# Two 128x256 matmuls in place of each 128x512 matmul of the three MLPs

## The chip, the cores and the metric

The kernel runs on one core of a Trainium2 chip (eight cores, one used). The metric is the device time of one execution in microseconds (us), taken as the median of several runs. A program is slower or faster here only if its time moves by more than about 0.2%, which is 4.6 us.

## What is computed

The reference is two small transformer blocks, one after the other, in float32, on 512 tokens of width 1024. The first block has an RWKV-7 recurrence beside differential attention, then a cross attention to 256 memory tokens, then an MLP. The second has two layers: a gated linear attention with an MLP, and a sliding-window attention with an MLP. The change touches only the three MLPs, which all have this form:

```python
D_FF = 4 * D_MODEL            # 4096
hn = rms_norm(h, norm_mlp_w[l])
h = h + jnp.square(jax.nn.relu(hn @ w_up[l])) @ w_down[l]
```

So each MLP is a product [512 x 1024] x [1024 x 4096], a squared ReLU, and a product [512 x 4096] x [4096 x 1024].

## The kernel before

**Layout.** Activations lie transposed: 128 features on the partitions, 512 tokens (`T`) along the row, with `KT` = 8 such tiles for a width of 1024. A matmul takes a 128x128 tile of the weights as its stationary operand and 128x512 of the activations as its moving operand, and adds 128 output features for all 512 tokens into one PSUM bank (128x512 float32, a whole bank). There are four banks `M[0..3]` for such products.

**Precision.** Each float32 operand is split in two parts, `_hi` and `_lo`, of the type fp32r. `exact3` (L1079 to L1082) makes one product from three matmuls: w_hi x x_hi, w_lo x x_hi, w_hi x x_lo. So a *triple* of matmuls stands for one 128x128 tile of weights.

**Weights.** SyncE loads the weights in blocks of 256 columns for eight k-tiles (1 MB) into a ring of four `raw` buffers (L964). ScalarE makes `w_hi` of a block (L1390), VectorE makes `w_lo` (L1606), each in a ring of two.

**The MLP on TensorE** (`mlp`, from L1128). It goes over the hidden width in two halves (loop `half`). In each half, first the up stage: a hardware loop `j` of two turns, four blocks of weights in each, two chunks `c` of 128 columns in each block. A chunk is eight k-tiles of three matmuls, that is 24 matmuls into one bank, from `f_hi` and `f_lo`, and its last matmul increments `acc_done`. VectorE then takes the ReLU out of the bank (L1677), ScalarE squares it (L1433) and makes `u_hi` (L1435), VectorE makes `u_lo` (L1680). Then the down stage: a hardware loop `q` of two turns with four blocks each; a bank takes 24 matmuls in a block for k-group 0, and 24 more in a later block for k-group 1, before VectorE adds it to `h` (L1692, L1701). On each engine the code's order is the order of work; TensorE waits for semaphores at the start of a block (`block_ready`, weights split) and of a chunk (`bank_free`, bank emptied).

All in all an MLP has 2 halves x (2 turns x 4 blocks x 2 chunks + 2 turns x 4 blocks x 2 chunks) x 24 = 1536 matmuls, and the three have 4608.

**Other matmuls that the prediction speaks of.** `chunk` is the same scheme outside the MLPs; for the memory tokens it runs with 256 tokens, `blocks(N_MK, 4, m_hi, m_lo, ..., tok=MEM)`. `block_tm` (matmuls L1113 to L1115) turns the roles round: 128 tokens of the activations are stationary and 256 columns of the weights move. `mem_scores` calls `exact3` with the queries `mq` stationary and 256 memory tokens `mk` moving, into one half of a bank and then the other. `norm_stat` (L1122) sums squares with a 128x512 matmul before each MLP.

Of the kernel before, what the change touches and what calls it, by code (L numbers as in the profile page):

```python
# [19 lines left out]
P = 128  # L20
T = 512
D = 1024
KT = D // P
# [88 lines left out]
def acc_before(n):  # L112

    return 2 * n - 16 * sum(n >= m + 32 for m in (N_MLP1, N_MLP2, N_MLP3))
# [20 lines left out]
def program(nc, A, out):  # L135
# [4 lines left out]
    with ctx:  # L140
# [17 lines left out]
        def at(off, name, shape, dt=f32):  # L158
            nbytes = 4 * int(np.prod(shape[1:]))
            t = nc.alloc_sbuf_tensor_at(name, shape, dt, offset=off[0])  # L160
            off[0] += (nbytes + 31) // 32 * 32
            return t
# [4 lines left out]
        w_hi = at(o, "w_hi", [P, 2, KT, BW], f32r)  # L167
        w_lo = at(o, "w_lo", [P, 2, KT, BW], f32r)
# [136 lines left out]
        def C(name, rows=slice(0, P)):  # L305
            a, n = CONST[name]
            return cst[rows, a:a + n]
# [756 lines left out]
        def _(pe):  # L1064
            mm = nc.tensor.matmul

            def wait(name, v):
                pe.wait_ge(S[name], v)

            def bank_free(k, r=None):  # L1070

                if k >= 4:
                    pe.wait_ge(S["acc_evac"], k - 3 if r is None else k - 3 + r)
                return M[k % 4]

            def block_ready(n, r=None):
                pe.wait_ge(S["w_lo_ready"], n + 1 if r is None else n + 1 + r)

            def exact3(dst, wh, wl, xh, xl, start, stop):  # L1079
                mm(dst, wh, xh, start=start, stop=False)  # L1080
                mm(dst, wl, xh, start=False, stop=False)  # L1081
                return mm(dst, wh, xl, start=False, stop=stop)  # L1082

            def chunk(n, c, hi, lo, first=None, cols=P, tok=T, inc=1, lo_sem="x_lo", order=range(KT)):

                if c == 0:
                    block_ready(n)
                k = acc_before(n) + c
                dst = bank_free(k)
                for i, kt in enumerate(order):  # L1090
                    if first is not None:
                        wait(lo_sem, first + i + 1)
                    ws = slice(c * P, c * P + cols)
                    last = exact3(dst[0:cols, 0:tok], w_hi[:, n % 2, kt, ws], w_lo[:, n % 2, kt, ws],
                                  hi[:, kt, 0:tok], lo[:, kt, 0:tok], i == 0, i == KT - 1)
                last.then_inc(S["acc_done"], inc)
# [31 lines left out]
            def mlp(n, first, nth):  # L1128
                f_hi, f_lo, u_hi, u_lo = mem_of[nth]
                k = acc_before(n)  # L1130
                with pe.Fori(0, 2) as half:
                    with pe.Fori(0, 2) as j:
                        for b in range(4):
                            block_ready(n + b, half * 16 + j * 4)
                            for c in range(2):
                                dst = bank_free(k + 2 * b + c, half * 24 + j * 8)
                                for kt in range(KT):
                                    if b == 0 and c == 0:
                                        wait("x_lo", first + kt + 1)
                                    ws = slice(c * P, c * P + P)  # L1140
                                    last = exact3(dst[:], w_hi[:, (n + b) % 2, kt, ws], w_lo[:, (n + b) % 2, kt, ws],
                                                  f_hi[:, kt, :], f_lo[:, kt, :], kt == 0, kt == KT - 1)
                                last.then_inc(S["acc_done"], 1)
                    with pe.Fori(0, 2) as q:
                        for b in range(4):
                            kg = b // 2
                            m = n + 8 + b
                            block_ready(m, half * 16 + q * 4)

                            pe.wait_ge(S["up_lo"], 32 * nth + 8 * kg + 8 + half * 16)  # L1150
                            for c in range(2):
                                kk = k + 16 + 2 * (b % 2) + c
                                dst = M[kk % 4] if kg else bank_free(kk, half * 24 + q * 4)
                                for kt in range(KT):
                                    ws = slice(c * P, c * P + P)
                                    last = exact3(dst[:], w_hi[:, m % 2, kt, ws], w_lo[:, m % 2, kt, ws],
                                                  u_hi[:, kg * 8 + kt, :], u_lo[:, kg * 8 + kt, :],
                                                  kg == 0 and kt == 0, kg == 1 and kt == KT - 1)
                                last.then_inc(S["acc_done"], 1)


# [1 line left out]
            for g in range(4):  # L1163
                wait(f"ld_x{g}", 16)
                for c in (2 * g, 2 * g + 1):
                    if c >= 4:
                        wait("xt_ev", c - 3)
                    for t in range(TT):
                        last = nc.tensor.transpose(X[c % 4][:, t * P:t * P + P], xt[:, t, c * P:c * P + P], C("ident"))
# [25 lines left out]
            for u in range(16):  # L1195
# [4 lines left out]
                for m in range(2):  # L1200
                    r = slice(64 * m, 64 * m + 64)
                    last = mm(X[m][:, 0:nk], dq[r, hd, qb * P:qb * P + P], dk[r, hd, 0:nk], start=True, stop=True)
# [11 lines left out]
                for kb in range(qb + 1):  # L1214
                    last = nc.tensor.transpose(X[2][:, kb * P:kb * P + P], de[1][:, kb * P:kb * P + P], C("ident"))
# [4 lines left out]
                for kb in range(qb + 1):  # L1220
                    last = mm(X[3][:, qb * P:qb * P + P], dv[:, kb, hd * P:hd * P + P], da_t[:, kb, :],  # L1221
                              start=kb == 0, stop=kb == qb)
# [13 lines left out]
            for g in range(4):  # L1236
                for i in range(2):
                    for t in range(2):
                        c = 2 * g + i
                        last = nc.tensor.transpose(X[g][:, i * MEM + t * P:i * MEM + t * P + P],  # L1240
                                                   mrow[:, t, c * P:c * P + P], C("ident"))
# [29 lines left out]
            for hd in range(4):  # L1271
# [5 lines left out]
                for t in range(2):  # L1277
                    for qb in range(4):
                        last = nc.tensor.transpose(X[2 + t][:, qb * P:qb * P + P], me[hd % 2][:, qb, t * P:t * P + P],
                                                   C("ident"))  # L1280
# [5 lines left out]
                for i in range(2):  # L1286
                    for t in range(2):
                        wait("ma_pt_lo", 2 * hd + t + 1)
                        f = slice((2 * hd + i) * P, (2 * hd + i) * P + P)
                        last = exact3(M[i], mv_hi[:, t, f], mv_lo[:, t, f], pt_hi[:, t, :], pt_lo[:, t, :],  # L1290
                                      t == 0, t == 1)
# [3 lines left out]

            norm_stat(2)
            mlp(N_MLP1, 16, 0)
            norm_stat(3)

            gla_pe(pe, mm, wait, chunk, blocks, block_tm, norm_stat)  # L1300
            norm_stat(5)
            mlp(N_MLP2, 32, 1)


# [37 lines left out]
            for c in range(KT):  # L1342
# [5 lines left out]
                for qb in range(4):  # L1348
# [7 lines left out]
                    for i in range(2):  # L1356
                        for kb in kbs:
                            last = mm(M[c % 2][64 * i:64 * i + 64, qb * P:qb * P + P],  # L1358
                                      sv[:, qb - 1 + kb, (c // 4) * 64:(c // 4) * 64 + 64],
                                      spt[u % 2][:, 2 * i + kb, :], start=kb == kbs[0], stop=kb == 1)  # L1360
                    last.then_inc(S["sw_pv"], 1)
            wait("sw_lo", KT)
            blocks(N_SOUT, 4, s_hi, s_lo)
            norm_stat(7)
            mlp(N_MLP3, 56, 2)
            norm_stat(8)

# [3 lines left out]
            for t in range(TT):  # L1371
                for half in range(2):
# [3 lines left out]
                    for c in range(4):  # L1376
                        last = nc.tensor.transpose(X[2 + i % 2][:, c * P:c * P + P], h[:, 4 * half + c, t * P:t * P + P],
                                                   C("ident"))
# [585 lines left out]
```

## Time and profile before

| | |
|---|---|
| median of 3 runs | 2297.1 us (2295.41 to 2300.19) |
| span of the profiled execution, first to last instruction | 2294.3 us |
| TensorE busy with matmuls / with weight loads | 2113.8 us (92%) / 1704.6 us (74%) |
| VectorE, ScalarE, GpSimd busy | 1006.4 us (44%), 744.2 us (32%), 114.5 us (5%) |
| mean granted TensorE clock | 0.953 of full speed |
| matmuls recorded | 13074, of them 4608 in the MLPs |

The time of the profiled execution itself is not listed beside its span; the span is 2.8 us under the median of the runs. A matmul and the loading of its weights are one instruction in the program and two records in the trace: PE is the matmul, PEld the weight load. Records of matmuls overlap, since they are pipelined: one of 395 ns starts every 232 ns. So the pace of a stretch is read from start times, and not from durations. A few matmul records are missing from the trace, so counts are taken from the loops where they matter.

### The profile page before, as it was taken

What the parts mean: (1) busy time and instruction counts of PE and PEld (TensorE: products, weight loads), DVE (VectorE), ACT (ScalarE), POOL (GpSimd) and SP (SyncE); (2) the same over time, 40 slices, a digit from 0 to 9 for tenths busy, and PEclk for the clock granted to TensorE, in tenths of its full rate; (3) what the DMA queues carried; (4) which work ended last, traced back from release to release, by engine and by line L of the source; (5) the groups of instructions that cost most, each with busy time, mean ns of one, the idle gap of its engine ahead of it and who ended that gap; (6) DMA issues with size and microseconds to landing.
All of it is one profiled execution on the core that took longest, in us unless ns stands there. A gap on an engine that the chain in (4) does not pass through costs nothing.

```text
span 2294.3 us, 31118 instructions
## 1 busy us (share of the span) xinstructions
PE 2113.8 (92%) x13074; PEld 1704.6 (74%) x13074; DVE 1006.4 (44%) x1274; ACT 744.2 (32%) x1083; POOL 114.5 (5%) x85
## 2 busy tenths in 40 slices
PE   6998688889989999997989899999999789999997
PEld 5865477669777888884787778888888567888885
DVE  4365355356444423425443444324343644423433
ACT  3132333244233312323322333223232553312321
POOL 2044000000000000002000000000000310000000
PEclk8999599989999999997999999999999799999999
DMA  6211000025262232221221022222232012222220
GB/s 193 92 56 55 1 3 3 3 74 167 80 90 88 92 110 91 92 74 55 92 92 56 19 86 97 92 91 92 91 124 93 5 37 92 92 92 91 92 92 37
DMA packets 167206, 176.22 MB, mean 77 GB/s; under 512 B 4045, under 2 KB 164838, under 8 KB 167105
## 3 DMA queue, kind: packets, MB, share of 16 engines
q1 hardware_dynamic: 165072, 167.79, 22.6%
q0 software_dynamic: 2032, 6.98, 1.9%
q8 instruction: 76, 1.25, 0.2%
q14 instruction: 26, 0.21, 0.0%
HBM read 169.51 MB, written 5.24 MB: 76 GB/s over the span
## 4 chain that ended last, share of the span: by engine, by line
PE 87%; DVE 6%; ACT 5%; issue 1%; DMA 0%; POOL 0%; SPq 0%; DVEq 0%; ACTq 0%
PE M L1080 23%; PE M L1081 23%; PE M L1082 23%; PE M L1113 1%; PE M L1115 1%; PE M L1114 1%; PE X L452 1%; PE M L452 1%; PE M L1358 1%; ACT sc L1573 1%; ACT mt L500 1%; PE X L1335 1%; PE X L1221 1%; PE X L760 1%; DVE h L1661 1%
## 5 line engine op out<-in xcount | busy, mean ns | idle before, releaser
L1606 DVE TENSOR_TENSOR w_lo<-raw,w_hi 128x2048 fp32r<-128x2048 f32 x155 | 353.2, 2278 | 364.9 <-ACT w_hi L1390 364.9
L1390 ACT ACTIVATE w_hi<-raw 128x2048 fp32r<-128x2048 f32 x155 | 293.6, 1895 | 407.9 <-PE M L1082 364.0
L1080 PE MATMUL M<-f,w_hi 128*128 128x512 f32 x768 | 304.6, 397 | 0.0
L1081 PE MATMUL M<-f,w_lo 128*128 128x512 f32 x768 | 303.4, 395 | 0.0
L1082 PE MATMUL M<-f,w_hi 128*128 128x512 f32 x768 | 303.3, 395 | 0.0
L1082 PE MATMUL M<-u,w_hi 128*128 128x512 f32 x768 | 303.1, 395 | 0.0
L1081 PE MATMUL M<-u,w_lo 128*128 128x512 f32 x768 | 303.1, 395 | 0.0
L1080 PE MATMUL M<-u,w_hi 128*128 128x512 f32 x768 | 303.1, 395 | 0.0
L1080 PEld LDWEIGHTS M<-f,w_hi 128*128 128x128 f32 x768 | 144.8, 189 | 35.4 <-issue 1.3
L1081 PEld LDWEIGHTS M<-f,w_lo 128*128 128x128 f32 x768 | 144.7, 188 | 34.8 <-issue 0.5
L1082 PEld LDWEIGHTS M<-f,w_hi 128*128 128x128 f32 x768 | 144.7, 188 | 34.2
L1081 PEld LDWEIGHTS M<-u,w_lo 128*128 128x128 f32 x768 | 144.5, 188 | 34.3
L1080 PEld LDWEIGHTS M<-u,w_hi 128*128 128x128 f32 x768 | 144.5, 188 | 34.2
L1082 PEld LDWEIGHTS M<-u,w_hi 128*128 128x128 f32 x768 | 144.5, 188 | 34.1
L1433 ACT ACTIVATE nt<-ut 128x512 f32<-128x512 f32 x96 | 60.7, 632 | 323.6 <-DVE ut L1677 323.6
L1680 DVE TENSOR_TENSOR u<-nt,u 128x512 f32 x96 | 66.5, 692 | 153.3 <-ACT u L1435 153.3
L1399 ACT ACTIVATE nt<-h 128x512 f32<-128x512 f32 x72 | 45.5, 631 | 246.2 <-DVE h L1630 112.2
L1677 DVE SCALAR_TENSOR_TENSOR ut<-M,rstd 128x512 f32<-128x512 f32 x96 | 66.1, 688 | 105.2 <-PE M L1082 105.0
L1080 PE MATMUL M<-gx_hi,w_hi 128*128 128x512 f32 (+1 forms) x200 | 82.2, 411 | 15.4 <-DVE gx_lo L1643 9.9
L1080 PE MATMUL M<-xm_hi,w_hi 128*128 128x512 f32 x176 | 72.6, 412 | 10.2 <-issue 10.2
L1082 PE MATMUL M<-gx_lo,w_hi 128*128 128x512 f32 (+1 forms) x200 | 81.8, 409 | 0.0
L1081 PE MATMUL M<-gx_hi,w_lo 128*128 128x512 f32 (+1 forms) x200 | 81.7, 409 | 0.0
(483 smaller groups left out, 3342.6 us busy)
## 6 DMA issues: line engine op xcount, KB each, us to landing
raw<-in_w_up_dram SPq DMA_DIRECT2D x48, 1024.0 KB, 5.3
raw<-in_w_down_dram SPq DMA_DIRECT2D x48, 1024.0 KB, 5.1
raw<-in_w_in_dram SPq DMA_DIRECT2D x14, 1024.0 KB, 5.4
raw<-in_a_w_in_dram SPq DMA_DIRECT2D x12, 1024.0 KB, 5.4
raw<-in_w_out_dram SPq DMA_DIRECT2D x4, 1024.0 KB, 5.0
raw<-in_w_mk_dram SPq DMA_DIRECT2D x4, 1024.0 KB, 5.0
raw<-in_w_mv_dram SPq DMA_DIRECT2D x4, 1024.0 KB, 5.2
raw<-in_w_mq_dram SPq DMA_DIRECT2D x4, 1024.0 KB, 5.1
```

The source lines that it names most:

```text
L452: last = mm(blk(bank, hh, cp, cpar), a_, b_, start=True, stop=True)
L500: nc.scalar.activation(out_, in_, func, **kw).then_inc(S["rw_act"], 1)
L760: last = mm(X[2 + hd // 2][:, (hd % 2) * 256:(hd % 2) * 256 + 256], gkt[cp % 2][r, hd, :], gv[r, cp, hd * 256:hd * 256 + 256], start=True, ...
L1080: mm(dst, wh, xh, start=start, stop=False)
L1081: mm(dst, wl, xh, start=False, stop=False)
L1082: return mm(dst, wh, xl, start=False, stop=stop)
L1390: nc.scalar.activation(w_hi[:, n % 2, :, 0:cols], raw[:, n % 4, :, 0:cols], ACT.Copy).then_inc(S["w_hi_ready"], 1)
L1399: nc.scalar.activation(b_[:, 0:tok], src, ACT.Square).then_inc(S[sem[0]], 1)
L1433: nc.scalar.activation(us[c][:], ut[c][:], ACT.Square).then_inc(S["up_sq"], 1)
L1606: TTO(w_lo[:, n % 2, :, 0:cols], raw[:, n % 4, :, 0:cols], w_hi[:, n % 2, :, 0:cols].bitcast(f32), ALU.subtract).then_inc(S["w_lo_ready"], 1)
L1677: STT(ut[c][:], M[(k + i) % 4], 0.0, rstd[:], ALU.max, ALU.mult).then_inc(S["acc_evac"], 1)
L1680: TTO(u_lo[:, u_, :], us[c][:].unsqueeze(1), u_hi[:, u_, :].bitcast(f32), ALU.subtract).then_inc(S["up_lo"], 1)
```

## The change

Each matmul of the MLPs over 512 tokens becomes two, over tokens 0 to 255 and 256 to 511. Each of the two has its own weight load. In the up stage the loop over the token halves `tk` lies outside the loop over the k-tiles: 24 matmuls into the first half of the bank and then 24 into the second. In the down stage it lies inside: three matmuls into the first half of the bank, three into the second, for each k-tile. There, only the very first matmul into a bank has `start` set. Semaphores, banks, loads and the other engines' code stay as they are.

```diff
-            def exact3(dst, wh, wl, xh, xl, start, stop):
-                mm(dst, wh, xh, start=start, stop=False)
-                mm(dst, wl, xh, start=False, stop=False)
-                return mm(dst, wh, xl, start=False, stop=stop)
+            def exact3(dst, wh, wl, xh, xl, start, stop, **kw):
+                mm(dst, wh, xh, start=start, stop=False, **kw)
+                mm(dst, wl, xh, start=False, stop=False, **kw)
+                return mm(dst, wh, xl, start=False, stop=stop, **kw)
...
-                                for kt in range(KT):
-                                    if b == 0 and c == 0:
-                                        wait("x_lo", first + kt + 1)
-                                    ws = slice(c * P, c * P + P)
-                                    last = exact3(dst[:], w_hi[:, (n + b) % 2, kt, ws], w_lo[:, (n + b) % 2, kt, ws],
-                                                  f_hi[:, kt, :], f_lo[:, kt, :], kt == 0, kt == KT - 1)
+                                for tk in (slice(0, 256), slice(256, T)):
+                                    for kt in range(KT):
+                                        if b == 0 and c == 0:
+                                            wait("x_lo", first + kt + 1)
+                                        ws = slice(c * P, c * P + P)
+                                        last = exact3(dst[:, tk], w_hi[:, (n + b) % 2, kt, ws], w_lo[:, (n + b) % 2, kt, ws],
+                                                      f_hi[:, kt, tk], f_lo[:, kt, tk], kt == 0, kt == KT - 1)
...
                                 for kt in range(KT):
-                                    ws = slice(c * P, c * P + P)
-                                    last = exact3(dst[:], w_hi[:, m % 2, kt, ws], w_lo[:, m % 2, kt, ws],
-                                                  u_hi[:, kg * 8 + kt, :], u_lo[:, kg * 8 + kt, :],
-                                                  kg == 0 and kt == 0, kg == 1 and kt == KT - 1)
+                                    for tk in (slice(0, 256), slice(256, T)):
+                                        ws = slice(c * P, c * P + P)
+                                        last = exact3(dst[:, tk], w_hi[:, m % 2, kt, ws], w_lo[:, m % 2, kt, ws],
+                                                      u_hi[:, kg * 8 + kt, tk], u_lo[:, kg * 8 + kt, tk],
+                                                      kg == 0 and kt == 0 and tk.start == 0, kg == 1 and kt == KT - 1,
+                                                      skip_group_check=True)
```

TensorE's instructions in the up stage of the first MLP, at the end of its first chunk (`f_0` is `f_hi`, `f_1` is `f_lo`; the REGISTER_ALU at L1073 works out what `bank_free` of the next chunk waits for). Before:

```order
L1080 MATMUL M<-f_0_142,w_hi 128x512
L1081 MATMUL M<-f_0_142,w_lo 128x512
L1082 MATMUL M<-f_1_143,w_hi 128x512
L1073 REGISTER_ALU
L1080 MATMUL M<-f_0_142,w_hi 128x512
```

And at the same place now:

```order
L1080 MATMUL M<-f_0_142,w_hi 128x256
L1081 MATMUL M<-f_0_142,w_lo 128x256
L1082 MATMUL M<-f_1_143,w_hi 128x256
L1080 MATMUL M<-f_0_142,w_hi 128x256
L1081 MATMUL M<-f_0_142,w_lo 128x256
```

After the 24th matmul the 25th follows, the first one over the other token half, and the next chunk comes only after the 48th. Nothing moves on the other engines, and SyncE's list is the same.

## Rows read from the trace of the kernel before

**Rows 1.** The page: TensorE's line, the chain that ended last, the MLP matmuls.
```profile
PE 2113.8 (92%) x13074; PEld 1704.6 (74%) x13074; DVE 1006.4 (44%) x1274; ACT 744.2 (32%) x1083; POOL 114.5 (5%) x85
...
PE 87%; DVE 6%; ACT 5%; issue 1%; DMA 0%; POOL 0%; SPq 0%; DVEq 0%; ACTq 0%
...
L1080 PE MATMUL M<-f,w_hi 128*128 128x512 f32 x768 | 304.6, 397 | 0.0
```

**Rows 2.** Busy time in the MLPs: engine us (instructions), granted clock, DMA share, GB/s.
```profile
705.60:1065.00 359.40, 357.30 (x1537) 289.31 (x1536) 129.64 (x119) 104.39 (x106) 0.00 (x0) 1.00 0.28 91
1353.80:1712.00 358.20, 358.20 (x1538) 290.00 (x1537) 133.48 (x122) 109.65 (x112) 0.00 (x0) 1.00 0.29 94
1915.00:2275.70 360.70, 358.55 (x1537) 288.14 (x1535) 129.41 (x118) 104.20 (x105) 0.00 (x0) 1.00 0.25 82
```

**Rows 3.** Timeline of TensorE: an early and the last matmul of each MLP.
```profile
706.03 0.39 PE L1081 MATMUL M<-f,w_lo 128*128 128x512 f32 x1
...
1062.50 0.40 PE L1082 MATMUL M<-u,w_hi 128*128 128x512 f32 x1
...
1356.18 0.39 PE L1081 MATMUL M<-f,w_lo 128*128 128x512 f32 x1
...
1711.94 0.40 PE L1082 MATMUL M<-u,w_hi 128*128 128x512 f32 x1
...
1915.22 0.39 PE L1081 MATMUL M<-f,w_lo 128*128 128x512 f32 x1
...
2273.15 0.40 PE L1082 MATMUL M<-u,w_hi 128*128 128x512 f32 x1
```

**Rows 4.** Waits in the first MLP: who waited for whom, us, times, longest.
```profile
ACT w_hi L1390 <- PE M L1082: 105.7, 12, 9.3
DVE ut L1677 <- PE M L1082: 34.4, 17, 2.6
```

**Rows 5.** Timeline: memory keys, 256 tokens moving, weights stationary (`chunk`).
```profile
531.89 0.28 PE L1080 MATMUL M<-m_hi,w_hi 128*128 128x256 f32 x1
...
544.81 0.28 PE L1080 MATMUL M<-m_hi,w_hi 128*128 128x256 f32 x1
```

**Rows 6.** Timeline: memory values (`block_tm`), around the wait at 550.7 us.
```profile
549.90 0.28 PE L1115 MATMUL M<-w_hi,m_lo 128*128 128x256 f32 x1
...
550.58 0.28 PE L1115 MATMUL M<-w_hi,m_lo 128*128 128x256 f32 x1
550.73 0.38 PE L1113 MATMUL M<-w_hi,m_hi 128*128 128x256 f32 x1
...
551.07 0.28 PE L1115 MATMUL M<-w_hi,m_lo 128*128 128x256 f32 x1
...
552.83 0.28 PE L1115 MATMUL M<-w_hi,m_lo 128*128 128x256 f32 x1
```

**Rows 7.** Tiles xm_hi and gx_hi in `block_tm`: duration ns, first and last start.
```profile
L1114 PE MATMUL M<-w_lo,xm_hi x64: 279/279/279, 76.8 to 99.1; 128*128 128x256 f32 x64
...
L1113 PE MATMUL M<-w_hi,gx_hi x80: 279/281/285, 1166.8 to 1194.9; 128*128 128x256 f32 x80
```

**Rows 8.** Timeline: `mem_scores`, one half of a bank after the other.
```profile
616.17 0.28 PE L1081 MATMUL X<-mk_hi,mq_lo 128*128 128x256 f32 x1
...
618.93 0.28 PE L1080 MATMUL M<-mk_hi,mq_hi 128*128 128x256 f32 x1
```

**Rows 9.** Timeline: 128 columns moving (`block_tm` of the shared keys and values).
```profile
1721.80 0.27 PE L1113 MATMUL M<-w_hi,kx_hi 128*128 128x128 f32 x1
...
1722.81 0.28 PE L1113 MATMUL M<-w_hi,kx_hi 128*128 128x128 f32 x1
```

**Rows 10.** Timeline: end of the first turn of loop `j`; entry to the MLP.
```profile
705.54 0.19 PEld L1080 LDWEIGHTS M<-f,w_hi 128*128 128x128 f32 x1 [0.41 <-issue]
...
750.18 0.39 PE L1082 MATMUL M<-f,w_hi 128*128 128x512 f32 x1
750.41 0.39 PE L1080 MATMUL M<-f,w_hi 128*128 128x512 f32 x1
```

## The prediction

> **What bounds the kernel now.** I read the page first. TensorE has matmuls in flight for 92% of the span, and the chain that ended last is TensorE for 87% [rows 1]. Then the busy time by stage: in the three MLPs, 1078 us of the 2294 us, matmuls are in flight 357 to 359 us out of 358 to 361, the clock is at its full level (1.00, that is 2.4 GHz), VectorE is busy 36% and ScalarE 30% [rows 2]. Nobody is ahead of TensorE there: in the waits of the first MLP ScalarE waits 105.7 us for it before it may split new weights, and VectorE waits 34.4 us for finished banks [rows 4]; no wait of TensorE stands inside an MLP. So a nanosecond more or less on each MLP matmul goes straight into the time, and all else of this change can hide. What must be known is the pace, start to start.
>
> **The pace with 512 columns.** From the second matmul of the first MLP to its 1536th are 1534 steps: (1062.50 - 706.03) / 1534 = 0.2324 us [rows 3]. In the second MLP the first row shown is the fifth matmul (a cold start lies before it): 355.76 / 1531 = 0.2324. In the third: 357.93 / 1534 = 0.2333. Over all 4608: 1536 x (0.2324 + 0.2324 + 0.2333) = 1072.3 us. These quotients hold 24 turns of the hardware loops, 192 chunks' waits and all weights, and still no step stands out: at the end of the first turn of `j` the next matmul starts 0.23 us after the last [rows 10].
>
> **What the change removes.** 4608 matmuls of 512 columns, at 1072.3 us. Nothing else: no load, no wait, no evacuation.
>
> **What it adds.** 9216 matmuls of 256 columns, with twice the weight loads. Their pace is the whole question. Break-even is 1072.3 / 9216 = 0.1164 us. The kernel already runs such matmuls, at full clock, in five places:
> - Memory keys, `chunk` with 256 tokens: 38 triples from 531.89 to 544.81, 12.92 / 114 = 0.1133 us [rows 5].
> - Memory values, `block_tm`: 6 steps in 0.68 us, 0.1133, up to the wait; 15 steps from 551.07 to 552.83, 0.1173, behind it [rows 6].
> - First projections, `block_tm`: 63 triples, 22.3 / 189 = 0.1180 [rows 7].
> - Gated attention, `block_tm`: 79 triples, 28.1 / 237 = 0.1186 [rows 7].
> - Memory scores, `exact3` into one half of a bank and then the other: 23 steps in 2.76 us, 0.1200 [rows 8].
>
> With 128 columns a step still takes 1.01 / 9 = 0.1122 us [rows 9]. There the moving operand is half as long and the step hardly shorter, so 0.112 us is what a weight load of 128 columns needs, and that is the floor below which no 256-column step can go. With 512 columns the load lies under the matmul with room to spare; with 256 the two are as long as each other, and the step is whatever their interplay makes it: from 0.1133 to 0.1200 in these rows. The break-even lies inside.
>
> Which value? Nearest by its code is the row at 0.1133: weights stationary, tokens moving, L1080 to L1082 as in the MLP. But `mem_scores` is the same function too and stands at 0.1200, and it alone writes the two halves of a bank in turn every few matmuls, as the new down stage does every three. And the memory values ran at 0.1133 and, behind one short wait, with the same code and the same tiles, at 0.1173 for good [rows 6]. So the pace seems to be something that the pipeline settles into at a start, and four of the five places settled at or above 0.117 sooner or later. I take 0.1180, the middle of these and the pace of the cleanest long stretch. Then 9216 x 0.1180 = 1087.5 us, **+15.2 us**. The ends are 9216 x 0.1133 = 1044.2 (-28.1 us) and 9216 x 0.1200 = 1105.9 (+33.6 us); they are kept for the range.
>
> Here the Trainium skill has a rule against the change. The page "TensorE: Matmul & The Clock Gate", section "Back-to-back issue gap", gives a warm step as the columns over 2.4 GHz plus about 2.5 ns. By it each added matmul costs 2.5 ns, an estimate of 11.5 us slower in all: the same sign as my sum and near its size. The trace does not bear out the rule's own figure for 512 columns, 216 ns against 0.2324 us measured.
>
> **What hides.** The other engines' work is the same in amount. A block of weights takes TensorE 48 x 0.2324 = 11.2 us now and 11.3 us then, and VectorE needs about 36% of it [rows 2]; even at 0.1133 (10.9 us) that stays far off. The banks go by the last matmul of a chunk as before, so the half that is ready earlier helps nobody. The ends of turns and the semaphore waits of a chunk cost nothing now; TensorE has half the time per instruction to cover them, and the memory keys cross four borders of chunks of 24 such matmuls at an unbroken 0.1133 us [rows 5], so I cost them at nothing. If the cover were gone, the entry to the MLP shows a price: 0.41 us of waiting for the issue [rows 10], times 24 turns, 10 us. The clock stays at its full level as matmuls stay gapless.
>
> **Sum.** Against the profiled span: 2294.3 + 15.2 = 2309.5 us. The median of the runs stands 2.8 us above that span, so the forecast is 2297.1 + 15.2 = 2312 us.
>
> **The rivals.**
> - *The quick pace holds (faster).* The MLPs settle at 0.1133 as the memory keys did, and stay there, since nothing in an MLP makes TensorE wait: 2297.1 - 28 = 2269 us. For it: same operands, same function, and a stretch of 13 us with chunk borders that never left the pace. Against it: the four other places. It decides in each MLP from the first microseconds on, wherever the step is under 0.1164. Chance 0.30.
> - *Mixed.* Some MLPs or stages (the up stage writes one half 24 times, the down stage alternates) settle at 0.1133 and others at 0.118. One MLP of three at the quick pace gives 2297.1 + (15.2 x 2 - 28.1) / 3 = 2298 us, two give 2297.1 + (15.2 - 28.1 x 2) / 3 = 2283 us. Chance 0.15.
> - *The pace of the scores everywhere.* 0.1200, for the changes of bank half: 2297.1 + 33.6 = 2331 us. Chance 0.11.
> - *The covers fall* at the turns of the loops, on top of 0.1180: 2312 + 10 = 2322 us. Against it: no mark now. Chance 0.03.
> - *Loads that no longer lie under matmuls.* Each added matmul would then cost a bare load of 0.112 us, 4608 x 0.112 = 516 us, 2813 us. The rows at 256 columns exclude it almost: a step of 0.113 to 0.120 us has no room for a load of 0.112 beside the streaming. Chance 0.01. The same page's Part 3 (row and column tiling) says that a weight load overlaps a running matmul only if its row group differs; the trace says otherwise, since all these tiles use all 128 rows and overlap.
>
> **How the numbers follow.** The forecast of 2312 us, with a pace between 0.1165 and 0.1190, has 0.40. Its own range is 2298 to 2322 us (9216 x 0.1165 and 0.1190 against 1072.3). Cases of both signs hold most of the chance, so the range must reach both ends: down to 2268 for the quick pace, up to 2334 for the pace of the scores. What lies outside (covers lost on top of 0.1200, bare loads, a pace outside the five) is under 0.1. A measurement of this kernel tells about 0.2%, 4.6 us, from no change. Faster: the quick pace 0.30 and half of the mixed case 0.08, 0.38. The same: the rest of the mixed case and the lower edge of the forecast, 0.09. Slower: 0.53.
>
> **What would show it.** In the profile after, the steps of L1080 to L1082 on `f` and `u` by their start times: 0.118 bears the forecast out, 0.1133 the first rival, 0.1200 the third. The stages must then last 9216 / 3 x the pace, 362.5 us each at 0.118. Weight loads should be in flight for all of each MLP, against 80% now (289 of 359 us). A gap at every 384th matmul would be the turns; a wait of TensorE for `w_lo` or a bank inside an MLP would prove the part on what hides wrong. A pace that changes within an MLP, or differs between up and down, would be the mixed case.

## The result, and the profile after

The changed kernel takes 2315.96 us (median of 4 runs, 2314.7 to 2324.16), the kernel before beside it 2296.26 us (4 runs, 2291.27 to 2300.19): a ratio of 1.0093, with a 95% interval of 1.0073 to 1.0114, **19.7 us slower**. The profiled execution of the changed kernel is the longest of its four, 2324.16 us, with a span of 2322.0.

The page of the changed kernel: TensorE's line, the shares of the chain, the MLP matmuls (busy us, mean ns of one, idle before them).

```profile
PE 2144.6 (92%) x17682; PEld 1941.6 (84%) x17682; DVE 1006.6 (43%) x1274; ACT 744.0 (32%) x1083; POOL 114.5 (5%) x85
...
PE 87%; DVE 6%; ACT 5%; issue 1%; DMA 0%; POOL 0%; SPq 0%; DVEq 0%; ACTq 0%
...
L1080 PE MATMUL M<-f,w_hi 128*128 128x256 f32 x1536 | 435.8, 284 | 0.0
```

These answer to [rows 1]: 4608 matmuls and weight loads more, VectorE and ScalarE unchanged, TensorE the bound as before. The busy time of each engine in the three MLPs (stretch, PE busy, PEld, DVE, ACT, POOL, granted clock, DMA share, GB/s), to be laid beside [rows 2]:

```profile
706.90:1077.00 370.10, 370.09 (x3074) 369.37 (x3072) 127.69 (x116) 103.78 (x105) 0.00 (x0) 1.00 0.28 88
1366.00:1731.00 365.00, 365.00 (x3075) 364.88 (x3074) 133.48 (x122) 109.64 (x112) 0.00 (x0) 1.00 0.29 92
1933.80:2300.10 366.30, 366.30 (x3074) 366.19 (x3072) 127.38 (x115) 103.55 (x104) 0.00 (x0) 1.00 0.25 80
```

Weight loads are in flight for the whole of each MLP (369.37 of 370.10 us, against 289 of 359), VectorE and ScalarE work as long as before, and no MLP has an idle stretch on TensorE. So nearly all of the added time is in the pace. The timeline of TensorE, an early (warm) and the last matmul of each MLP, as in [rows 3]:

```profile
709.03 0.28 PE L1081 MATMUL M<-f,w_lo 128*128 128x256 f32 x1
...
1076.71 0.28 PE L1082 MATMUL M<-u,w_hi 128*128 128x256 f32 x1
...
1366.43 0.28 PE L1081 MATMUL M<-f,w_lo 128*128 128x256 f32 x1
...
1730.74 0.28 PE L1082 MATMUL M<-u,w_hi 128*128 128x256 f32 x1
...
1937.63 0.28 PE L1082 MATMUL M<-f,w_hi 128*128 128x256 f32 x1
...
2300.02 0.28 PE L1082 MATMUL M<-u,w_hi 128*128 128x256 f32 x1
```

Of the 3072 matmuls of an MLP, the first rows shown are the 8th, the 2nd and the 18th. First MLP: (1076.71 - 709.03) / 3064 = 0.1200 us. Second: 364.31 / 3070 = 0.1187. Third: 362.39 / 3054 = 0.1187. Break-even was 0.1164. The pace is the same in the up stage, in the down stage and across the turns of the loops.

**Where the 27.7 us of span went.** At these paces the 9216 matmuls take 3072 x (0.1200 + 0.1187 + 0.1187) = 1098 us against 1072.3 before: 25.7 us. About 1.5 us more is a start of the third MLP at the lower level of the clock (1.2 GHz), with steps of 0.21 us until the 17th matmul at 1937.44; about 1 us went in the same way into the first seven steps of the first MLP (2.08 us for 0.84). In the profile of before these two MLPs started at the full level. The second MLP was the other way about: before, its first four steps took 2.34 us (1353.84 to 1356.18) at the lower level, and in the changed kernel it started at the full level, which gave some 1.2 us back. So the starts together cost little more than 1 us, and the rest outside the MLPs some 0.5 us. In both kernels TensorE had been idle 2.64 or 2.65 us ahead of each MLP, for the norm, whichever way the start came out. The start of the third MLP, before and then after (columns as above, the clock third from the end):

```profile
1914.70:1925.00 10.30, 10.30 (x45) 8.26 (x44) 3.68 (x3) 4.39 (x5) 0.00 (x0) 1.00 0.28 90
```

```profile
1933.80:1944.00 10.20, 10.20 (x73) 10.10 (x72) 3.20 (x3) 4.38 (x5) 0.00 (x0) 0.83 0.28 84
```

**The profiled run and the median.** If all three MLPs run at 0.1187, the sum is 1093.9 us, +21.6; the first MLP's 0.1200 is 4 us more. That may be part of why the profiled execution lies 8 us over the median of the four; the other three were not profiled.

The waits in the first MLP, to be laid beside [rows 4]. The other two engines wait a little longer for TensorE than before, and TensorE for nobody:

```profile
ACT w_hi L1393 <- PE M L1082: 110.1, 12, 9.7
DVE ut L1680 <- PE M L1082: 40.8, 18, 2.8
```

### The profile page after: what moved, and what is told of

Its sections match the earlier page's. It is cut to its first block, busy times and chain, and to the rows that moved or that the text cites. A ratio compares the mean times of both kernels' runs of the same rounds, so it can differ in the third digit from the quotient of the medians.

```text
span 2322.0 us, 40334 instructions
## 1 busy us (share of the span) xinstructions
PE 2144.6 (92%) x17682; PEld 1941.6 (84%) x17682; DVE 1006.6 (43%) x1274; ACT 744.0 (32%) x1083; POOL 114.5 (5%) x85
## 4 chain that ended last, share of the span: by engine, by line
PE 87%; DVE 6%; ACT 5%; issue 1%; DMA 0%; POOL 0%; SPq 0%; DVEq 0%; ACTq 0%
PE M L1080 23%; PE M L1081 23%; PE M L1082 23%; PE M L1113 1%; PE M L1114 1%; PE M L1115 1%; PE X L452 1%; PE M L452 1%; PE M L1361 1%; ACT sc L1576 1%; ACT mt L500 1%; PE X L1224 1%; PE X L1338 1%; PE X L760 1%; DVE h L1664 1%
## 5 line engine op out<-in xcount | busy, mean ns | idle before, releaser
L1080 PE MATMUL M<-f,w_hi 128*128 128x256 f32 x1536 | 435.8, 284 | 0.0
L1081 PE MATMUL M<-f,w_lo 128*128 128x256 f32 x1536 | 435.0, 283 | 0.0
L1081 PE MATMUL M<-u,w_lo 128*128 128x256 f32 x1536 | 434.1, 283 | 0.0
L1080 PE MATMUL M<-u,w_hi 128*128 128x256 f32 x1536 | 433.6, 282 | 0.0
L1082 PE MATMUL M<-f,w_hi 128*128 128x256 f32 x1536 | 432.8, 282 | 0.0
L1082 PE MATMUL M<-u,w_hi 128*128 128x256 f32 x1536 | 432.0, 281 | 0.0
L1081 PEld LDWEIGHTS M<-f,w_lo 128*128 128x128 f32 x1536 | 290.6, 189 | 0.7 <-issue 0.5
L1080 PEld LDWEIGHTS M<-f,w_hi 128*128 128x128 f32 x1536 | 290.0, 189 | 1.3 <-issue 1.3
L1082 PEld LDWEIGHTS M<-f,w_hi 128*128 128x128 f32 x1536 | 291.0, 189 | 0.0
L1082 PEld LDWEIGHTS M<-u,w_hi 128*128 128x128 f32 x1536 | 290.0, 189 | 0.0
L1081 PEld LDWEIGHTS M<-u,w_lo 128*128 128x128 f32 x1536 | 289.5, 188 | 0.0
L1080 PEld LDWEIGHTS M<-u,w_hi 128*128 128x128 f32 x1536 | 289.0, 188 | 0.0
```

The source lines that it names most:

```text
L1080: mm(dst, wh, xh, start=start, stop=False, **kw)
L1081: mm(dst, wl, xh, start=False, stop=False, **kw)
L1082: return mm(dst, wh, xl, start=False, stop=stop, **kw)
```

## The experiments

The sign was as forecast, but a question stayed open: why did the memory keys take 0.1133 [rows 5] with the same function, engine and shapes? Below, the pace is (last - first start) / steps between; a row of one line of `exact3` holds every third matmul. Kernels A are edits of the changed kernel, kernels B of the kernel before. A time without an interval is one run.

### Is it the layout of the tiles, or the stage?

The keys' rows are 1 KB (256 tokens) in each k-tile, the MLP's are halves of 2 KB rows. **keys_wide** (A) gives the keys the MLP's row stride:

```diff
-        m_hi, m_lo = at(o, "m_hi", [P, KT, MEM], f32r), at(o, "m_lo", [P, KT, MEM], f32r)
+        m_both = at(o, "m_both", [P, KT, T], f32r)
+        m_hi, m_lo = m_both[:, :, 0:MEM], m_both[:, :, MEM:T]
```

> The changed kernel, with one edit outside the MLPs: the memory keys' moving operands m_hi and m_lo lie side by side in rows of 512 elements (2 KB from one k-tile to the next, as in the MLPs) instead of rows of 256 (1 KB). Theory 'layout': the memory keys owe their quick pace of 0.1133 us to their packed rows; with the wide rows they go to 0.118 to 0.120 us, 192 matmuls, +1 us in all. Theory 'start': the pace is what the pipeline settles into at a start and has nothing to do with the rows; the keys stay at 0.1133 us or take any of the other paces, and the MLPs, which are unchanged here, may come out at another pace than 0.1200 / 0.1187 / 0.1187 us.

Measured: 2318.55 us, the keys still at 0.1133 to 0.1135. The MLPs took 0.1187, 0.1200 and 0.1187, another order of the same two values as in the changed kernel's profile. So the stride is not the cause, and one MLP takes one value or the other from run to run.

**halves_apart** (A) gives the MLP the keys' layout: each token half of `f` and `u` contiguous (the writes on ScalarE and VectorE changed to match).

```diff
-            f = [at([arena + fo * KB + 16 * KB * i], f"f{nth}_{i}", [P, KT, T], f32r) for i in range(2)]
-            u = [at([arena + a * KB], f"u{nth}_{i}", [P, 16, T], f32r) for i, a in enumerate((uo, vo))]
+            f = [at([arena + fo * KB + 16 * KB * i], f"f{nth}_{i}", [P, 2, KT, 256], f32r) for i in range(2)]
+            u = [at([arena + a * KB], f"u{nth}_{i}", [P, 2, 16, 256], f32r) for i, a in enumerate((uo, vo))]
```

> The changed kernel with f and u stored with the two token halves apart, so that the moving operand of one k-tile lies 1 KB from the next, as with the memory keys, instead of 2 KB. ScalarE and VectorE write the same elements in two pieces per instruction. Theory 'layout': the MLPs run at 0.1133 us a matmul, 9216 x 0.1133 = 1044 us, and the kernel takes about 2297 - 28 = 2269 us, below the kernel before. Theory 'start': the pace stays among 0.1178 to 0.1200 us in most MLPs, and the kernel stays at 2310 to 2325 us.

Measured: 2311.73 us (2309.86 to 2316.56), ratio 1.0078 (1.0061 to 1.0094). All MLPs at 0.1187. The layout theory falls from both sides.

**up_only** and **down_only** (A) put back the old code of the down stage and of the up stage; the up stage fills one half of a bank for 24 matmuls, the down stage alternates every three. The edit of up_only:

```diff
-                                    for tk in (slice(0, 256), slice(256, T)):
-                                        ws = slice(c * P, c * P + P)
-                                        last = exact3(dst[:, tk], w_hi[:, m % 2, kt, ws], w_lo[:, m % 2, kt, ws],
...
+                                    ws = slice(c * P, c * P + P)
+                                    last = exact3(dst[:], w_hi[:, m % 2, kt, ws], w_lo[:, m % 2, kt, ws],
...
```

> Only the up stages are split in token halves; the down stages keep their 128x512 matmuls. If the cost is the same for each added matmul (0.1187 to 0.1200 us against half of 0.2324 to 0.2333), half of it is here: 10 to 14 us over the kernel before, the up stages at 0.1187 or 0.1200 us a matmul, the down stages at 0.2324 or 0.2333. If the alternation between the halves of a bank in the down stage were what costs (theory 'alternation'), the up stages alone would run at less than 0.1187 us and this kernel would stand within 5 us of before.

> Only the down stages are split; the up stages keep their 128x512 matmuls. Same cost for each added matmul: 10 to 14 us over the kernel before, the down stages at 0.1187 or 0.1200 us a matmul. Theory 'alternation': all of the 20 us is here. Theory 'start': a stage entered from a running stream of 512-column matmuls without a stop may settle at another pace than one entered from a stop, as the memory keys did (0.1133 us).

Measured: 2308.85 and 2317.77 us, 12.8 and 21.7 us over the 2296.04 of the kernel before (7 runs). The split up stages run at 0.1187 (once 0.1200), the split down stages at 0.1187 and 0.1200: no difference between one half and alternation. The 512-column stages beside them keep 0.2324 to 0.2333. The 21.7 us of down_only miss the 10 to 14 that were expected, and taken alone they would speak for the alternation. The stages do not: by the starts of the first and last matmul of each MLP the three took 16 us more than before, near the expected cost; the other 5 us of its span lie outside the MLPs (the first MLP starts at 712.7 us instead of 705.6), and this is one run.

In down_only the memory keys, whose code nobody touched, began at 0.1133 and went over to 0.1178. The tile `m_hi` in down_only, one of the three lines of the triple, first and then later (duration ns least, median, most; first to last start):

```profile
L1080 PE MATMUL M<-m_hi,w_hi x16: 276/276/384, 527.8 to 534.0; 128*128 128x256 f32 x16
...
L1081 PE MATMUL M<-m_hi,w_lo x27: 280/281/282, 539.8 to 549.0; 128*128 128x256 f32 x27
```

(549.0 - 539.8) / (3 x 26) = 0.1179. The timeline has the place: TensorE had waited 0.82 us for weights, and the steps are 0.1178 behind this wait. In halves_apart the keys went the other way at a wait, 0.1178 ahead of it and 0.1133 behind. First down_only, then halves_apart:

```profile
532.83 0.38 PE L1080 MATMUL M<-m_hi,w_hi 128*128 128x256 f32 x1 [0.82 <-DVE w_lo L1608]
```

```profile
523.01 0.39 PE L1080 MATMUL M<-m_hi,w_hi 128*128 128x256 f32 x1 [0.61 <-DVE w_lo L1612]
```

So the same stretch can take one of two discrete paces, and these two changes came at a new start of TensorE. The down stages of down_only also change between 0.1187 and 0.1200 without a wait, from one to the next, with a 512-column stage between them. What was left to differ between keys and MLP was where the operands lie in SBUF.

### The address of the moving operand against the stationary one

The function `at` rounds addresses to 32 bytes only. In the kernels before and after, modulo 256 (the remainder of the address by 256), the weights `w_hi` and `w_lo` lie at 128, `f`, `u` and `gx` at 0, `xm` and the keys' `m` at 64. Everything behind `arena` moves with one edit. **shift64**, **shift32**, **shift96** and **shift192** (A) and **whole_shift64** (B) are this line with 64, 32, 96, 192 and 64 bytes:

```diff
-        arena = o[0]
+        arena = o[0] + 64
```

Nothing else changes: the same instructions, each on the same shapes.

> The changed kernel with 64 bytes left free in SBUF ahead of everything that lies behind the weight buffers (arena = o[0] + 64): f, u, gx and x2 then lie at an address of 64 modulo 128 where they lay at 0, and the tiles xm, m, mk and mq go from 64 to 0. The weight buffers stay at 0. Theory 'address': so far every stretch whose stationary and moving operands differ by 64 modulo 128 (xm, m against w) ran at 0.1133 or 0.1178 us, and every stretch where they are alike (f, u, gx against w; mk against mq) ran at 0.1187 or 0.1200. So now the MLPs and the gated attention's values go to 0.1178 or 0.1133 us and the keys, the memory values and the first projections to 0.1187 or 0.1200; the scores stay at 0.1187 or 0.1200. Time: at 0.1178, 2297 + 13 = 2310 us; at 0.1133, 2269 us. Theory 'start': the set of paces does not follow the address: the MLPs stay at 0.1187 or 0.1200, the keys at 0.1133, and the kernel at 2312 to 2320 us.

> The same with 32 bytes: the MLPs' moving operands lie at 32 modulo 128 against weights at 0, and the keys' at 96. Theory 'address': both stretches go to paces of their own, the same in all three MLPs, and different from shift64 if 32 bytes count, or those of one of the two known sets if only 64 bytes count. Theory 'start': MLPs at 0.1187 or 0.1200, keys at 0.1133.

> The same with 96 bytes: MLPs at 96 modulo 128, keys at 32. Theory 'address': if the sign of the difference does not count, the MLPs run as in the run with 32 bytes. Theory 'start': MLPs at 0.1187 or 0.1200, keys at 0.1133.

> The kernel before (128x512 matmuls) with the same 64 bytes left free. The 512-column matmuls ran at 0.2323 or 0.2333 us with operands alike modulo 128 and at 0.2331 to 0.2334 with operands 64 apart. Theory 'address': the MLPs go to 0.2333 us or so, up to 3 us slower than before. Theory 'start': no change beyond 0.2323 or 0.2333 us from MLP to MLP. Both: a control for the run with 64 bytes, within 0.2% of the kernel before.

Measured, against before at 2297.0 us (19 runs): shift64 2281.14 us (10 runs, 2262.74 to 2293.24), ratio 0.9922 (0.9895 to 0.9949): an address made the split faster than the kernel before. shift32 2308.61, shift96 2320.56 us. whole_shift64 2299.84 (10 runs), ratio 1.002 (1.000 to 1.004). Tile `f` in the first MLP, from 720 to 780 us. The changed kernel, all three lines of the triple:

```profile
L1081 PE MATMUL M<-f,w_lo x168: 285/285/285, 719.8 to 780.0; 128*128 128x256 f32 x168
L1082 PE MATMUL M<-f,w_hi x167: 281/281/281, 720.0 to 779.7; 128*128 128x256 f32 x167
L1080 PE MATMUL M<-f,w_hi x167: 284/284/284, 720.1 to 779.8; 128*128 128x256 f32 x167
```

shift64, the last of these lines:

```profile
L1080 PE MATMUL M<-f,w_hi x177: 276/276/277, 720.0 to 779.8; 128*128 128x256 f32 x177
```

In the same 60 us 177 triples instead of 167; 59.8 / (3 x 176) = 0.1133, the pace of the keys. And the keys went the other way: now at 128, as the weights, they run at 0.1200 in shift64, and their duration is 283 ns:

```profile
L1080 PE MATMUL M<-m_hi,w_hi x57: 283/283/385, 522.1 to 543.0; 128*128 128x256 f32 x57
```

The 512-column matmuls on `xm`, which came to the same place modulo 256 as the weights, went from 0.2333 inside a chunk down to 0.2267 in both kernels with 64 bytes. Tile `gx_hi` and tile `xm_hi` in whole_shift64: the one, with a difference of 192, has durations from 393 to 398 ns; the other, with none, has 389 ns for every one.

```profile
L1080 PE MATMUL M<-gx_hi,w_hi x55: 393/397/398, 1201.9 to 1239.7; 128*128 128x512 f32 x55
```

```profile
L1080 PE MATMUL M<-xm_hi,w_hi x15: 389/389/389, 62.0 to 71.6; 128*128 128x512 f32 x15
```

That gave the theory of the last four runs: the pace goes by the difference of the two operands' addresses modulo 256, and 512 columns are quickest where it is zero.

### Everything aligned

**whole_align** (B) puts all activations at 128 modulo 256, as the weights; **split_align** (A) is the same edit on the changed kernel. **whole_align_w** (B) also moves the weights and all else on by 128 bytes, so that both lie at 0.

```diff
-        arena = o[0]
+        arena = o[0] + 128
...
-        mixing = o[0]
+        mixing = o[0] + 192
+        o = [mixing]
```

whole_align_w has this line more, ahead of `w_hi`:

```diff
+        o = [o[0] + 128]
```

> The kernel before (128x512 matmuls, no split) with free bytes in SBUF such that all activations lie at the same address modulo 256 as the weight buffers (128), 128 bytes ahead of the arena and 192 ahead of the tiles behind it. In the two runs with 64 bytes the first projections came to lie so, and their 512-column matmuls stepped at 0.2267 us instead of 0.2331. Theory 'address': all 512-column matmuls with 128x128 weights, MLPs included, go to 0.2267 us: 4608 x 0.0060 = 28 us in the MLPs and some 1500 x 0.0063 = 10 us outside, 2260 us in all, faster than any version so far and without the split. The 256-column stretches go to 0.1187 or 0.1200. Theory 'start': the 0.2267 us belongs to the first projections' start, the MLPs stay at 0.2323 or 0.2333 and the kernel at 2290 to 2300 us.

> The changed kernel (split MLPs) with the same placement as the run before it. Theory 'address': 256-column matmuls with operands alike modulo 256 step at 0.1200 us (memory keys and first projections did in the runs with 64 bytes), so the MLPs take 9216 x 0.1200 = 1106 us, 61 us more than the unsplit MLPs at 0.2267, and the kernel is at about 2321 us. Theory 'start': the MLPs stay at 0.1187 or 0.1200 whatever the placement, and the difference to the unsplit kernel stays at 20 us.

> As the first of these four, but the weight buffers moved by 128 bytes too, so that weights and activations all lie at 0 modulo 256. If it is the difference between the two operands' addresses that counts, the 512-column matmuls step at 0.2267 us again and the time is that of the first run, 2260 us. If it is the activations' own address that counts (0 modulo 256, as in the kernel before), they step at 0.2323 or 0.2333 us, 2297 us.

> The changed kernel with 192 bytes ahead of the arena: MLP activations 64 bytes behind the weights modulo 256, where the run with 64 bytes had them 64 ahead. The difference modulo 128 is the same. Theory 'address', only the difference modulo 128 counts: the MLPs at 0.1133 or, from an unlucky start, 0.1178 us, and 2262 to 2300 us as with 64 bytes. If the sign counts: another pace, the same in all MLPs. Memory keys and first projections lie at a difference of 128 modulo 256, as the MLPs of the changed kernel: 0.1187 or 0.1200 us for 256 columns and 0.2323 or 0.2333 for 512. Theory 'start': MLPs at 0.1187 or 0.1200.

Measured, against before at 2295.05 us (17 runs, 2287.27 to 2300.23):

| kernel | median us (range) | ratio to before (interval) | MLP pace us |
|---|---|---|---|
| whole_align | 2267.15 (2257.8 to 2273.79) | 0.9881 (0.9852 to 0.991) | 0.2267 |
| whole_align_w | 2266.55 (2260.0 to 2275.68) | 0.9889 (0.9857 to 0.9921) | 0.2267 |
| split_align | 2322.15 (2321.81 to 2322.76) | 1.0121 (1.0097 to 1.0145) | 0.1200 |
| shift192 | 2300.24 (2285.82 to 2309.05) | 1.001 (0.9987 to 1.0032) | 0.1178 |

Tile `f` from 720 to 780 us. The kernel before, whole_align, split_align, shift192, each one line of the triple:

```profile
L1080 PE MATMUL M<-f,w_hi x87: 390/393/404, 719.7 to 779.7; 128*128 128x512 f32 x87
```

```profile
L1083 PE MATMUL M<-f,w_hi x89: 389/389/389, 719.8 to 779.7; 128*128 128x512 f32 x89
```

```profile
L1083 PE MATMUL M<-f,w_hi x168: 283/283/283, 719.9 to 780.0; 128*128 128x256 f32 x168
```

```profile
L1082 PE MATMUL M<-f,w_hi x171: 279/279/279, 719.8 to 779.8; 128*128 128x256 f32 x171
```

Before, the 512-column matmul has durations from 390 to 404 ns and a step of 60.0 / 258 = 0.2326. Aligned, every one lasts 389 ns and the step is 59.9 / 264 = 0.2269. The alignment brings 2295.05 - 2267.15 = 28 us on the kernel before with no instruction changed, and 4608 x (0.2327 - 0.2267) = 28 us is what the MLPs alone should bring (the 512-column matmuls outside them gain too, the 256-column ones lose). whole_align_w gives the same time with the weights at 0, so it is the difference that counts, not where either lies. And aligned, the split costs 2322.15 - 2267.15 = 55 us: 9216 x 0.1200 - 4608 x 0.2267 = 61 us by the paces.

**whole_align is faster than both kernels of this case**, by 28 us than the one before and by some 49 us than the changed one.

The expectation for whole_align was 2260 us, 7 under its median. Three of its six runs took 2257.8 to 2262.53 us, the other three 2271.77 to 2273.79.

All profiles together, with the *moving* operand's address less the *stationary* one's, modulo 256. In `block_tm` the weights move and the activations are stationary, so the sign turns there.

| difference | 256 columns, us | where | 512 columns, us |
|---|---|---|---|
| 0 | 0.1200 | scores [rows 8]; keys in shift64; all of split_align | 0.2267 |
| 64 | 0.1178, at some starts 0.1133 | `xm` and memory values [rows 6, 7]; `gx` in shift64; MLPs in shift192 | 0.2289 |
| 128 | 0.1187, at some starts 0.1200 | MLPs after; `gx` [rows 7] | 0.2323 to 0.2333 |
| 192 | 0.1133, at some starts 0.1178 | keys [rows 5]; MLPs in shift64; `gx` in shift192 | 0.2333 |

The tile `gx_hi` in `block_tm` is the one that had the two values with its sign turned: shift64 (difference 64) first, then shift192 (difference 192).

```profile
L1113 PE MATMUL M<-w_hi,gx_hi x63: 280/280/280, 1167.9 to 1189.8; 128*128 128x256 f32 x63
```

```profile
L1113 PE MATMUL M<-w_hi,gx_hi x86: 276/276/415, 1167.8 to 1196.9; 128*128 128x256 f32 x86
```

21.9 / 186 = 0.1177 and 29.1 / 255 = 0.1141 (a short wait lies in it). Differences of 160 (shift32) and 224 (shift96) lie between: 0.1173 and about 0.1183 with 256 columns, 0.2343 and 0.2334 with 512.

That the remainder by 128 would not do shows in the right-hand column: 0 and 128 give 0.2267 and 0.2323 to 0.2333, 64 and 192 give 0.2289 and 0.2333. And 256 is enough: in whole_align `xm` lies at the same place as the weights modulo 512 too, `f` and `gx` 256 bytes off, and all step at 0.2267.

**What stays open.** The mechanism behind the addresses is not shown, only the rule that these runs follow. The tiles of VectorE and ScalarE moved along with TensorE's; that TensorE's two operands are what counts rests on different tiles (keys, `xm`, `gx`, MLPs), with different work beside them, that fall on the same line of the table. What makes a start take the one value of its row or the other is not shown either: the first MLP of the changed kernel at 0.1200 and of keys_wide at 0.1187, the keys of down_only and halves_apart that change at a wait.

Nor is the spread of the medians settled, since only one execution of each kernel was profiled (shift64 2274.05 and whole_align 2262.53 us, all MLPs at 0.1133 and at 0.2267). The granted clock is on record for every execution, and in part it goes with the time. The ten of whole_shift64 run from 2295.46 us at a mean clock of 0.954 to 2308.99 at 0.947, almost in order. In whole_align the three quicker ones had 0.950 to 0.957 and the others 0.946, 0.946 and 0.950. It does not explain the split kernels: shift64 took 2262.74 us at 0.955 and 2280.92 at 0.956, shift192 2285.82 and 2309.05, both at 0.954. That such executions held another pace in some MLP is a guess; the estimate for one MLP at 0.1178 instead of 0.1133 is 3072 x 0.0045 = 14 us. So is the reason why the split costs 55 us by the medians when aligned and 59 us by the profiled spans (2319.7 and 2260.4). That the steps of two 256-column matmuls at 192 and of one aligned 512-column matmul are equal, 2 x 0.1133 = 0.2267, was not followed up.

## Why the prediction was right

The measured median of 2316 us lies 4 us over the forecast of 2312, within the likeliest case's own range (2298 to 2322). What bounds the kernel and the form of the sum were right. The sign was luck in part: it hangs on where the tiles lie, which the prediction never asked, and 64 bytes ahead of the arena turn it (shift64).

- **What bounds the kernel: right.** TensorE was busy for the whole of each MLP, and kernels that only moved tiles changed the time with the same instructions (shift64 by 35 us against the changed kernel, whole_align by 28 against the one before).
- **The pace before, and break-even: right.** Break-even was 0.1164 us, and all three MLPs came out above it.
- **The pace of 256 columns, 0.1180: mis-sized by 1%.** It measured 0.1187 in two MLPs and 0.1200 in one. Close to break-even that 1% weighs much: at 0.1187 the term is +21.6 us and not +15.2, and at the paces of the profiled execution +25.7. The reason for taking 0.1180, "the middle of these and the pace of the cleanest long stretch", chose `xm`, with a difference of 64. The row that the MLPs share their difference of 128 with was the gated attention's 0.1186 [rows 7], which lay in the same group.
- **"The pace seems to be something that the pipeline settles into at a start": half right.** Behind a new start a stretch may have another pace, but only one of the few that go with its addresses. The places read in the profile of before cover all four differences of the table. The rival of the quick pace got 0.30 for "same operands, same function"; it failed since the keys have a difference of 192 and the MLPs one of 128. With the MLPs moved to 192 it comes true: shift64, ratio 0.9922.
- **The pace of the scores at 0.1200 "for the changes of bank half": wrong reason.** The down stage changes halves every three matmuls and the up stage every 24, and both ran at 0.1187 in the second MLP and at 0.1200 in the first. `mk` and `mq` have difference 0, and split_align, all at 0, runs at 0.1200 throughout.
- **What hides: right.** VectorE and ScalarE are busy as long as before and wait longer; loop turns and chunks cost nothing. The clock stayed at its full level once an MLP ran; which MLPs start at 1.2 GHz differed between the two profiles (the first and third after, the second before), for about 1 us in all.
- **The floor of 0.112 us: it held as a bound.** The quickest 256-column step of any run is 0.1133. That 0.112 us is the time of the weight load itself stays an estimate from [rows 9]; no run separates it.
- **The Trainium skill's rule** ("TensorE: Matmul & The Clock Gate", "Back-to-back issue gap") gave the right sign and, with its estimate of 11.5 us, about half of what the paces cost. Its cost per matmul is one number, and the runs have no such number: by the address alone the split costs 55 us (split_align against whole_align), 20 us (as written), or wins 19 us (shift64 against whole_shift64).

## What to carry to other kernels

Read the pace of a dense matmul stretch from start times, and when two stretches with the same instructions differ by a few per cent, compare the operands' addresses modulo 256 before the code. A kernel bound by 512-column fp32r matmuls is worth one run with moving and stationary tiles at the same place modulo 256; it was 1.2% here and cost a few hundred bytes in each partition. A change that looks like a loss or a gain of 1% may be only where the new tiles came to lie, so move the allocation by 64 bytes before judging it.

## What the runs showed of the hardware

- The step of a full-clock fp32r matmul depends on the SBUF address of the moving against the stationary operand modulo 256 bytes: 0.2267 to 0.2343 us with 512 columns, 0.1133 to 0.1200 with 256. The two widths rank the differences nearly opposite: 0 is the best for 512 and the worst for 256.
- Two of the paces can be read from the duration in one row: 276 ns goes with 0.1133 and 389 ns with 0.2267. The others can't, and need start times: 0.1200 at a difference of 0 has 283 ns on all three lines of the triple in split_align's first MLP, but 280 to 287 in its second, and 279 to 282 ns occur at 0.1178 and at 0.1187.
- Where a difference has two values, one start takes one for hundreds of microseconds (each MLP of the changed kernel, more than 360 us), and the next run may take the other. The changes looked at lie at waits of 0.82 us (down_only) and 0.61 us (halves_apart), and where 512-column stages come between (down_only).
